# The last three slots of an output, not two, take the first token tile ahead of the second (sublayers 0 to 3)

## What is computed

```
def _ffn_sublayer(h, mod, g_pre, g_post, w_in, w_out):
    shift, scale, gate = mod
    u = _modulate(_rmsnorm(h, g_pre), shift, scale)
    a, b = jnp.split(u @ w_in, 2, axis=-1)
    y = (jax.nn.silu(a) * b) @ w_out
    return h + MACARON_W * gate * _rmsnorm(y, g_post)
```

## Time and profile before

| | |
|---|---|
| median of 3 runs | 2883.66 us (2882.22 to 2893.26) |
| the profiled execution | 2885.18 us, of it span 2883.4 us |
| PE busy (matmul) | 2779.8 us, 96% of the span |
| DVE busy | 1935.4 us, 67% |
| ACT busy | 1507.3 us, 52% |
| mean granted clock of PE | 0.993 of full speed |

### The profile page before, as it was taken

One profiled execution on the slowest core, in us unless ns is written; L12 is line 12 of the kernel. 1 busy time (PEld: TensorE's weight loads), 2 busy tenths in 40 slices (PEclk: granted clock), 3 DMA queues, 4 the chain that ended last, 5 costly groups with the idle time before them and its releaser, 6 DMA issues.

```text
span 2883.4 us, 35254 instructions
## 1 busy us (share of the span) xinstructions
PE 2779.8 (96%) x13616; PEld 2285.0 (79%) x13616; DVE 1935.4 (67%) x2518; ACT 1507.3 (52%) x2286; POOL 135.7 (5%) x132
## 2 busy tenths in 40 slices
PE   6999999989999999999999999999899999998999
PEld 5887888667888888878886788887688888896787
DVE  7888786777788797765545654655665554686654
ACT  5454465686454454544555644544754444476543
POOL 0000000000000000000040000000000000193000
PEclk9999999999999999999999999999999999999999
DMA  8667684306677677875462355554355555550553
GB/s 334 222 238 274 229 253 157 106 14 250 219 266 265 202 290 269 289 243 185 175 236 80 120 193 188 200 179 171 126 203 178 188 202 186 180 176 1 205 183 130
DMA packets 100550, 562.56 MB, mean 195 GB/s; under 512 B 20256, under 2 KB 20768, under 8 KB 43936
## 3 DMA queue, kind: packets, MB, share of 16 engines
q1 hardware_dynamic: 100384, 560.30, 55.5%
HBM read 559.17 MB, written 1.09 MB: 194 GB/s over the span
## 4 chain that ended last, share of the span: by engine, by line
PE 76%; DVE 8%; ACT 5%; DMA 4%; issue 4%; POOL 3%; SPq 0%; DVEq 0%; POOLq 0%; ACTq 0%
PE banks L364 20%; PE banks L365 20%; PE banks L814 14%; PE banks L912 6%; PE banks L369 3%; PE banks L370 3%; PE banks L371 3%; POOL od_glu L2161 2%; DVE ada_terms L445 2%; PE banks L852 2%; DVE w_rest L348 2%; DMA w_raw<-in_w_ffn_in 1%; POOL normed L2157 1%; ACT w_high L338 1%; DMA ada_tiles<-in_w_ada 1%
## 5 line engine op out<-in xcount | busy, mean ns | idle before, releaser
L348 DVE TENSOR_TENSOR w_rest<-w_raw,w_high 128x2048 fp32r<-128x2048 f32 x426 | 976.0, 2292 | 537.6 <-ACT w_high L338 536.4
L338 ACT ACTIVATE w_high<-w_raw 128x2048 fp32r<-128x2048 f32 x426 | 810.8, 1907 | 211.6 <-PE banks L912 143.9
L364 PE MATMUL banks<-w_high,u_parts 128*128 128x512 f32 x1888 | 748.1, 396 | 8.2 <-DVE u_parts L735 7.1
L365 PE MATMUL banks<-w_high,u_parts 128*128 128x512 f32 x1888 | 737.6, 391 | 0.0
L814 PE MATMUL banks<-w_rest,u_parts 128*128 128x512 f32 x1856 | 498.7, 391 | 4.5 <-DVE w_rest L348 4.5
L364 PEld LDWEIGHTS banks<-w_high,u_parts 128*128 128x128 f32 x1888 | 356.0, 189 | 80.5 <-issue 9.4
L365 PEld LDWEIGHTS banks<-w_high,u_parts 128*128 128x128 f32 x1888 | 356.2, 189 | 71.1
L814 PEld LDWEIGHTS banks<-w_rest,u_parts 128*128 128x128 f32 x1856 | 349.0, 188 | 79.1 <-DVE w_rest L348 5.4
L364 PE MATMUL banks<-w_high,gated_high 128*128 128x512 f32 x968 | 378.9, 391 | 0.0
L365 PE MATMUL banks<-w_high,gated_rest 128*128 128x512 f32 x968 | 376.8, 389 | 0.0
L880 ACT ACTIVATE gated_high<-banks 128x512 fp32r<-128x512 f32 x121 | 72.5, 599 | 420.0 <-PE banks L852 419.7
(11 more groups left out here) (295 smaller groups left out, 2958.4 us busy)
## 6 DMA issues: line engine op xcount, KB each, us to landing
w_raw<-in_w_ffn_in SPq DMA_DIRECT2D x242, 1024.0 KB, 4.8
w_raw<-in_w_ffn_out SPq DMA_DIRECT2D x121, 1024.0 KB, 4.8
ada_tiles<-in_w_ada SPq DMA_DIRECT2D x128, 512.0 KB, 4.6
w_raw<-in_w_mix SPq DMA_DIRECT2D x54, 1024.0 KB, 4.8
w_raw<-in_w_mix_out SPq DMA_DIRECT2D x22, 1024.0 KB, 4.8
ada_first<-in_w_ada SPq DMA_DIRECT2D x7, 1024.0 KB, 14.9
post_gain_row<-post_mod SPq DMA_DIRECT2D x10, 512.0 KB, 6.3
na_bias<-in_na_bias SPq DMA_DIRECT2D x1, 4096.0 KB, 14.2
```

What stands on the lines that cost most here:

```text
L338: act.activation(w_high(g)[:, 0:n], raw[:, g % RING, 0:n], ACT.Copy).then_inc(w_hi_ready, 1)
L348: nc.vector.tensor_tensor(w_rest(g)[:, 0:n], raw[:, g % RING, 0:n], w_high(g)[:, 0:n].bitcast(F32), ALU.subtract).then_inc(w_lo_ready, 1)
L364: nc.tensor.matmul(ps, hi_a, hi_b, start=first_, stop=False)
L365: nc.tensor.matmul(ps, lo_a, hi_b, start=False, stop=False)
```

## The change

One number: `hold` is 3 instead of 2 for s < 4. For s >= 4 it is 3 before and after.

```
-HOLD = 2, 3
+HOLD = 3, 3
```

## The result

| | before | after |
|---|---|---|
| median | 2883.66 us (7 runs, 2879.24 to 2894.92) | 2898.99 us (7 runs, 2895.31 to 2903.77) |
| profiled execution, its span | 2885.18 us, 2883.4 us | 2895.31 us, 2893.5 us |
| PE busy | 2779.8 us | 2782.2 us |

The ratio is 1.0054, interval 1.0036 to 1.0071: the change makes the kernel 15.6 us slower (the medians are 15.3 us apart). That lies a hair over the 0.5% that was called measurable, and the interval reaches to both sides of it. The time is inside the predicted range (2886 to 2902). The forecast said +10.3 us and no change that counts. The two profiled executions are 10.1 us apart. That the profiles give the forecast and the medians do not is the question of the experiments.

The account below looks back on a forecast made before the run. PE bounds the kernel (busy 2779.8 of 2883.4 us), with DVE the second bound at output ends. Terms 3.5 + 3.2 + 3.55 + 0.2 + 1.0 - 1.2 + 0 = +10.25 us on the 2883.66 median give 2894 us, range 2886 to 2902.

Parts of the forecast that it names:

- The chain of DVE: Ends of out2x and out2c: a later freed buffer delays DVE's gapless chain and then PE, +3.5 and +3.2 us.
- out2x: End of this output: DVE idles before the rest of next[0], PE waits for post work and gates, +3.5 us.
- out2c: End of this output: same delay as out2x, passing in full to PE, +3.2 us.
- out0x: End of this output: the rest of next[0] begins later and all of it reaches PE, +3.55 us.
- The mixer: out1x, out1c and the start of in2x: 5.0 us late, partly given back there, +1.0 us stays.
- out3x: This output: longer waits for slots 9 and 10, less a wait and low clock behind it, -1.2 us.
- out0c: This output: the buffer comes free a few tenths behind the transfer the high part waited for, +0.2 us.
- 4.4 us of relief: Start of in2x and behind out3x: waits of 2.27 and 2.24 us and 1.73 us low clock each, largely given back.
- falls of the clock in five places: Two in out1c, gates of out2x and out2c, last of out3x: 8.7 us more if all fell; rival's chance 0.2.
- The swallowed delay: Rival: overlooked slack of DVE or PE absorbs delays at the ends, +5 us or less, 2884 to 2889; chance 0.15.
- The earlier tile 0: Rival: post work starts sooner and waits at the ends go, 11.2 us in all, 2872.5 us; chance 0.03.
- a granted clock of 0.5 behind the new waits: Sign that the prediction is wrong: low clock showing behind PE's new waits, worked out as 1.7 to 2.0 us.

Follow-up runs that it names:

- E3: Kernel before with three held slots only in the two outputs of sublayer 2 (x and ctx): ratio 1.0024, 6.9 us slower.
- E4: Changed kernel with tile 0's post work put ahead of the next pass's first slot in the ACT and DVE lists: ratio 1.0015, 4.3 us over the kernel before.
- E6: Changed kernel with sums of modulation tiles moved away from output ends in sublayers 2 and 3: ratio 1.0047, 13.6 us over the kernel before.
- E12: Kernel before with three held slots only in out3x: ratio 1.0017, 4.9 us slower.
- E11: Kernel before with three held slots only in out0x: ratio 1.0020, 5.8 us slower.
- E10: Changed kernel with DVE's sums at four output ends put behind the first gate products: ratio 1.0039, 11.2 us over the kernel before.
- E7: Kernel before (two held slots) with sums of modulation tiles moved away from output ends in sublayers 2 and 3: ratio 1.0005.
- E1: Kernel before again, no edit: median 2880.81 us in 11 runs, 2877.82 to 2889.69.

## Why the prediction was right, and where it was not

**The chain of DVE (out2x, out2c): right.** +3.5 and +3.2 were said, and 3.7 to 3.8 was measured at both in three profiles each. The idle DVE ahead of the rest of next[0] is 3.61 us (3.4 said), the waits are 1.80 and 1.51 (1.9 and 1.75 said). E3 shows the sum on the clock of the chip, E4 and E6 that it is the list and its length: with the post work in the idle time, or with sums taken out, the same freed buffer costs 0.6 us or less. For out2c, 3.2 was too small, in part since I left out that a held slot's rest is late there: PE's row at 1056.03 in the profile after waited 0.20 us for it, and the phase came 0.36 us late.

**out0x: right.** +3.55 against 4.2, 3.4, 3.5 and 3.3 in four profiles. Waits of 2.08 for `post_term` and 1.48 for the gates stand where 2.1 and 1.5 were said.

**The mixer and out3x: right against the profile, wrong as terms of the median.** Against the profile before, +1.0 and -1.2 were said, and -0.35 and -1.4 measured in the mean (as written, 2.7 - 2.1 - 1.7 is -1.1). The new waits of the profile after at out1c are 1.26 us for `normed` and 1.55 for `u_parts`, where 1.8 was said for each. In both, some 4 us of waits and low clock were to be given back. They are not there in every execution with two held slots. The wait in in2x is 0.7 to 2.4 us in seven profiles, with the low clock behind it in two (before and E12); the wait for a rest behind out3x is there in three of five (2.24, 2.41 and 1.70 us), with the low clock behind it in two (before and E3). On average the end of the mixer lies 2.0 us below the profile before, and that of out3x 2.4 us. Against the mean of executions the terms are +1.65 and +1.1, the second no clearer than zero.

**The sum.** 3.6 + 0.2 (out0c) + 1.65 + 3.7 + 3.7 + 1.1 = 14.0 us, against 15.3 between the medians and 10.3 said. The step that was off is the one from the profiled execution to the median: "On the median of 2883.66 that is 2894 us". It left in the sum 4.4 us of relief that an execution of the kernel before gives only if both waits and both falls of the clock are in it. The 10.1 us between the two profiled spans, which meet the forecast so well, are luck: that same execution, beside the fastest of seven of the changed kernel.

**The range.** That 2899 us lies in it is partly luck too. The forecast's own mechanism was given 2891 to 2897; the part above stood for falls of the clock in five places behind new waits. In the two profiles of the changed kernel none of these five places has a fall (one in E12 has, behind a wait of 2.09 us at 1239.11), so what filled that part was the relief that did not come.

**The rivals.** The swallowed delay is out: no end was made up for later. The earlier tile 0 did not pay; that it was queued behind the high part is shown by E4, where it comes first. But even there it pays nothing over the kernel before. The clock did fall behind a new wait, at in3x in the profile after. The prediction had named a granted clock of 0.5 behind the new waits as a sign that it is wrong, and this sign is there. PE's timeline and the windows (the granted clock is the last but two):

```profile
1078.08 0.47 PE L364 MATMUL banks<-w_high,u_parts 128*128 128x512 f32 x1 [1.81 <-DVE post_term L552]
...
1080.79 1.87 PE L814 MATMUL banks<-w_rest,u_parts 128*128 128x512 f32 x4
...
1085.50 0.65 PE L852 MATMUL banks<-identity,gated 128*128 128x128 f32 x4
```

```profile
1080.00:1082.00 2.00, 2.00 (x6) 1.60 (x5) 1.97 (x4) 2.00 (x3) 0.00 (x0) 0.50 0.45 184
```

Four matmuls took 1.87 us instead of 1.07, but the turn of the gates at 1085.50 then has no wait: the fall was swallowed by the next wait, as the prediction had said for this pair. The same happens behind out0x in E6 and E11, where the windows show the low clock from 237 and 236 us on, behind waits of 2.08 and 2.07 us, and PE then has no wait for the gates. So the sign came and the cost did not. What the 1.3 us between 14.0 and 15.3 are is open; it is within the scatter of both.

The bound of 0.5% was passed by a hair (1.0054, interval 1.0036 to 1.0071), a case that had been given 0.2, and for another reason than the one it stood for.

## What to carry to other kernels

A thing that becomes ready sooner is worth nothing while the engine that takes it stands, by its list, at something that the same change made later: move a consumer's list with the producer's order, or don't move either. A profile is one execution, so a term that gives back a wait which it shows must be weighed by how often that wait is there; the second profile of the unchanged kernel alone would have moved this forecast from 10 to 14 us. And work that is moved on one engine moves what the transfer queue issues behind it: in E10 loads waited for buffers that later sums freed, and in E6 and E7 a slow store came to stand among loads that had no slack.

## What the runs showed of the hardware that I had not expected

- The low clock is not tied to the length of a wait alone. At 1622.21 in E1's profile a wait of 1.91 us was followed by 1.2 GHz from 1623.5 (granted clock 0.50; the window from 1623 holds half of each level), while the same wait of 1.91 us at 1628.83 in the first profile was not the earlier trace rows. Behind a wait of 1.81 us the clock fell once (at in3x above); behind one of 2.14 us (in E3's profile, start of in2x) it did not.

```profile
1623.00:1624.00 1.00, 1.00 (x5) 0.82 (x4) 0.00 (x0) 0.97 (x3) 0.00 (x0) 0.75 0.76 246
1624.00:1625.00 1.00, 1.00 (x4) 0.81 (x3) 0.69 (x1) 1.00 (x4) 0.00 (x0) 0.50 1.00 418
```

- Most of the kernel's scatter goes with this: in eleven runs of E1 the time rises from 2878 to 2890 us as the mean clock falls from 0.994 to 0.989, and from 2893 to 2909 in the changed kernel (0.993 to 0.988, correlation -0.93). Not in every version: in E7 the correlation is only -0.35.
- The transfer of one gain row landed 1.6 us later against DVE's readiness in one execution than in another (DVE's wait 4.92 and 3.35 us), and with it PE's wait was 2.27 instead of 0.75 us. In all seven profiles with two held slots there, PE's wait is DVE's less 2.6 us (3.34 to 5.05 us for DVE, 0.74 to 2.44 us for PE).
- A store of 4 KB in some 1000 small packets (E6, at 1220.57 us) took 12.7 us to land, and loads of 512 KB issued around it took 12.5 us.
